# Expert lookup in two PSUM banks, and five edits where one block hands over to the next

## What is computed

```python
def adaln_norm(x, c, g, w_ada, b_ada):
    mod = jax.nn.silu(c) @ w_ada + b_ada
    shift, scale, gate = jnp.split(mod, 3, axis=-1)
    h = rms_norm(x, g) * (1.0 + scale[:, None, :]) + shift[:, None, :]
    return h, gate[:, None, :]

def peer(h, wq, subkeys, u_tab, v_tab):
    q = (xt @ wq).reshape(T, PEER_HEADS, 2, PEER_HALF)
    sc = jnp.einsum('thpd,hpkd->thpk', q, subkeys)
    vals, ids = lax.top_k(sc, PEER_TOPK)
    cand = (vals[:, :, 0, :, None] + vals[:, :, 1, None, :])
    cid = (ids[:, :, 0, :, None] * PEER_KEYS + ids[:, :, 1, None, :])
    top, pos = lax.top_k(cand, PEER_TOPK)
    idx = jnp.take_along_axis(cid, pos, axis=-1)
    g = jax.nn.softmax(top, axis=-1)
```

## Time and profile before

| | us |
|---|---|
| median of 3 runs | 2238.18 (2234.31 to 2246.16) |
| profiled execution | 2242.05 |
| its span, first to last instruction | 2240.2 |
| PE busy | 2175.6, 97% |
| DVE busy | 1571.8, 70% |
| POOL busy | 1241.3, 55% |
| ACT busy | 937.6, 42% |
| mean granted TensorE clock | 0.986 of 2.4 GHz |

### The profile page before, as it was taken

How to read it: one execution, slowest core, us unless ns; L and a number is a source line. 1 busy time by engine, 2 the same in 40 slices (tenths; PEclk the granted TensorE clock), 3 DMA queues, 4 the chain that set the end, 5 groups by cost and what they waited for, 6 DMA issues and landing times.

```text
span 2240.2 us, 32178 instructions
## 1 busy us (share of the span) xinstructions
PE 2175.6 (97%) x11877; PEld 1944.6 (87%) x11877; DVE 1571.8 (70%) x3061; ACT 937.6 (42%) x1541; POOL 1241.3 (55%) x670
## 2 busy tenths in 40 slices
PE   6999999999999999999999999999999999999999
PEld 6897989888888877888999999999998888888887
DVE  5736777685556755552999999999974766666665
ACT  3235576432455414432434334555553333333332
POOL 1634222375223341242588788766657787778775
PEclk9999999999999999999999999999999999999999
DMA  7252424222221440232488788999989999999995
GB/s 281 88 186 106 144 92 133 73 104 95 95 85 57 147 154 20 76 133 103 148 269 287 266 291 267 344 357 328 352 301 345 368 348 357 351 348 361 356 359 217
DMA packets 164476, 492.42 MB, mean 220 GB/s; under 512 B 15072, under 2 KB 64608, under 8 KB 162912
## 3 DMA queue, kind: packets, MB, share of 16 engines
q1 hardware_dynamic: 107872, 305.79, 39.3%
q0 software_dynamic: 36864, 134.23, 16.1%
q10 hardware_dynamic: 19584, 50.34, 5.9%
HBM read 437.87 MB, written 52.43 MB: 219 GB/s over the span
## 4 chain that ended last, share of the span: by engine, by line
PE 40%; DVE 9%; POOL 2%; DMA 1%; issue 1%; ACT 0%; DVEq 0%; ACTq 0%; POOLq 0%
PE ps L2566 22%; PE ps L2530 14%; PE ps L2548 4%; POOL t_split L2675 1%; DVE arena L2794 1%; DVE arena L2763 1%; DVE arena L2754 1%; DVE arena L2755 1%; DVE rope L2732 1%; DVE arena L2759 1%; DVE norm_rows L2732 1%; DVE arena L2789 1%; DVE arena L2732 1%; DVE arena L2750 1%; DVE arena L2797 0%
## 5 line engine op out<-in xcount | busy, mean ns | idle before, releaser
L2675 POOL TENSOR_TENSOR t_split<-t_raw,t_split 128x1024 fp32r<-128x1024 f32 x225 | 550.1, 2446 | 220.1 <-ACT t_split L2601 218.1
L267 POOL TENSOR_TENSOR w_split<-ring,w_split 128x1024 fp32r<-128x1024 f32 x113 | 274.3, 2428 | 490.9 <-ACT w_split L259 445.0
L2530 PE MATMUL ps<-h_hi,t_split 128*128 128x384 f32 x2048 | 537.4, 338 | 7.4 <-POOL t_split L2675 4.4
L2566 PE MATMUL ps<-t_split,w_split 128*128 128x512 f32 x2304 | 522.8, 389 | 3.1 <-DVE t_split L2849 1.6
L2566 PEld LDWEIGHTS ps<-t_split,w_split 128*128 128x128 f32 x2304 | 432.3, 188 | 93.5 <-DVE t_split L2849 2.0
L2601 ACT ACTIVATE t_split<-t_raw 128x1024 fp32r<-128x1024 f32 x256 | 270.3, 1057 | 340.2 <-PE ps L2566 304.0
L291 PE MATMUL ps<-h_hi,w_split 128*128 128x512 f32 x1280 | 402.6, 392 | 0.0
L2530 PEld LDWEIGHTS ps<-h_hi,t_split 128*128 128x128 f32 x2048 | 373.4, 189 | 10.1 <-POOL t_split L2675 6.6
L2530 PE MATMUL ps<-h_lo,t_split 128*128 128x384 f32 x1024 | 343.9, 336 | 0.0
L291 PEld LDWEIGHTS ps<-h_hi,w_split 128*128 128x128 f32 x1280 | 240.3, 188 | 50.5 <-issue 0.7
L291 PE MATMUL ps<-h_lo,w_split 128*128 128x512 f32 x640 | 249.1, 389 | 0.0
(11 more groups left out here) (367 smaller groups left out, 3333.3 us busy)
## 6 DMA issues: line engine op xcount, KB each, us to landing
ring<-w_stream SPq DMA_DIRECT2D x203, 512.0 KB, 3.4
t_raw<-u_table SPq DMA_DIRECT2D x128, 512.0 KB, 4.8
t_raw<-v_table SPq DMA_DIRECT2D x128, 512.0 KB, 5.6
gelu_scratch<-e_gel ACTq DMA_DIRECT2D x128, 192.0 KB, 4.8
gates_scratch<-arena ACTq DMA_DIRECT2D x8, 3072.0 KB, 13.4
arena<-gelu_scratch SPq DMA_DIRECT2D x32, 768.0 KB, 5.9
arena<-gates_scratch SPq DMA_DIRECT2D x32, 768.0 KB, 8.8
first<-w_stream SPq DMA_DIRECT2D x16, 512.0 KB, 13.3
```

What stands on the lines that cost most here:

```text
L267: pool.tensor_tensor(w_split[:, i % RS, 1, :], ring[:, n % R, :], w_split[:, i % RS, 0, :].bitcast(F32), ALU.subtract).then_inc(lo_done, 1)
L2530: mm = pe.matmul(ps[:, 6 + n % 2, 0:NT], t_split[:, n % RAWS, u, k * P:(k + 1) * P], h_parts[h][:, k, P:T], start=(k + u + h == 0), stop=( ...
L2566: mm = pe.matmul(ps[:, 2 * i + half, :], w_split[:, b % 2, w, at:at + P], t_split[:, m % RAWS, v, half * 512:(half + 1) * 512], start=(n + ...
L2675: pool.tensor_tensor(t_split[:, m % RAWS, 1, :], t_raw[:, m % RAWS, :], t_split[:, m % RAWS, 0, :].bitcast(F32), ALU.subtract).then_inc(t_ ...
```

## The change

It has these parts.

1. **Lookup**: the comparison and the product of the selection move from SBUF to banks 1 and 2 of PSUM (`match`), in place, in halves of 128 x 1024, with the comparison's 0..15 in bank 3. PE's turned selections all go to bank 0. The plan's prices go from 2.3, 2.3, 3.3 a pass to 1.2 a half pass.
2. **Shift's share**: DVE multiplies the weight piece with the shift and sums it over the tiles (`dve_share`, eight chained operations of 128 x 128, in SBUF), before it adds output unit 6; PE needs one matmul of one column instead of eight. The ring buffer of that piece waits for DVE's sum instead of PE's matmuls.
3. **Sums**: `pe_totals` runs inside the last output unit, ahead of its last two tiles; its part of DVE's chain is taken ahead (`dve_half`). The order of `dve_raw` moves up by one unit, and that of the raw products around the sums is changed.
4. **Two scaled tiles in PSUM**: tiles 2 and 3 of `dve_scale` go to bank 7 and to the bank of the shift; the copy of the shift's share comes between.
5. **`feature_group`** begins with the products of h's upper part and waits for the rest of h after them.
6. **Query norm**: the spreads, the rotations and one set of transposes in n2's phase come one unit later (spreads after units 7 to 9).
7. Two semaphores of one stage are merged into one (`f_dve`).

```diff
-                for k in range(KD):
-                    mm = pe.matmul(ps[:, self.shift_bank, 0:1], ring[:, n % R, k * P:(k + 1) * P],
-                                   self.shifts[:, k:k + 1], start=(k == 0), stop=(k == KD - 1))
-                mm.then_inc(self.turned.sem, 1)
+                self.share_summed.wait(pe, 1)
+                pe.matmul(ps[:, self.shift_bank, 0:1], share_sum, C("ones")[:, 0:1], start=True,
+                          stop=True).then_inc(self.turned.sem, 1)
...
+            def dve_share(self, dve):
+                n = self.raw_unit
+                dve.wait_ge(piece_in[n % R], 16 * (n // R + 1 - FIRST_PIECES // R))
+                for k in range(KD):
+                    block = ring[:, n % R, k * P:(k + 1) * P]
+                    if k == 0:
+                        ins = dve.tensor_scalar(share_sum, block, self.shifts[:, 0:1], None, ALU.mult)
+                    else:
+                        ins = dve.scalar_tensor_tensor(out=share_sum, in0=block, scalar=self.shifts[:, k:k + 1],
+                                                       in1=share_sum, op0=ALU.mult, op1=ALU.add)
+                    if k < KD - 1:
+                        dve.wait_ge(dve_step, note("dve", ins))
+                ins.then_inc(self.share_summed.sem, 1)
...
+            def scaled_tile(self, k):
+                if self.raw_unit is not None and k in (2, 3):
+                    return ps[:, 7 if k == 2 else self.shift_bank, :]
+                return ntmp[:, k, :]
...
-            if late:
-                for at in range(3):
+            if upper:
+                upper.wait(pe, 1)
+                for j in range(2):
+                    w[j] = piece_ready(pe, pieces[j])
+                    for a in range(2):
+                        pe.matmul(ps[:, banks[j], :], w[j][:, a, 0:P], src[0][:, 0, :], start=(a == 0), stop=False)
+                src_ready.wait(pe, 1)
+                for j in range(2):
+                    pe.matmul(ps[:, banks[j], :], w[j][:, 0, 0:P], src[1][:, 0, :], start=False, stop=False)
...
-                    feature_unit(pe, at + u, 4 + u % 3, h_parts)
+                    feature_unit(pe, at + u, 4 + u % 3, h_parts, pause=norm.pe_totals if u == KD - 1 else None)
...
-                    for v in {KD - 1: (KD - 3, KD - 2)}.get(u, (u - 2,) if u >= 2 else ()):
-                        norm.dve_raw(dve, v)
+                    if u >= 1:
+                        norm.dve_raw(dve, u - 1)
+                    if u == KD - 2:
+                        norm.dve_share(dve)
...
-                    for r in {6: (0, 1), 7: (2, 3), 8: (4,)}.get(u, ()):
+                    for r in {7: (0, 1), 8: (2, 3), 9: (4,)}.get(u, ()):
...
-                        step(dve.tensor_tensor(
-                            eq.rearrange("p h k a -> p (h k) a"),
-                            posab[:, j, :].unsqueeze(2).to_broadcast([P, P, PTOP]),
-                            C("iota16").unsqueeze(1).to_broadcast([P, P, PTOP]), ALU.is_equal))
-                        paced(2.3)
-                        step(dve.tensor_tensor(
-                            prod, eq, ids3[:, :, j, :].unsqueeze(2).to_broadcast([P, PH, PTOP, PTOP]), ALU.mult))
-                        paced(2.3)
-                        step(dve.tensor_reduce(sel[:, j, :], prod.rearrange("p h k a -> p (h k) a"), AX.X, ALU.add))
-                        paced(3.3)
+                        for half in range(2):
+                            of = slice(half * (P // 2), (half + 1) * (P // 2))
+                            heads = slice(half * (PH // 2), (half + 1) * (PH // 2))
+                            step(dve.tensor_tensor(
+                                match, posab[:, j, of].unsqueeze(2).to_broadcast([P, P // 2, PTOP]),
+                                iota_ps.unsqueeze(1).to_broadcast([P, P // 2, PTOP]), ALU.is_equal))
+                            paced(1.2)
+                            by_head = match.rearrange("p (h k) a -> p h k a", k=PTOP)
+                            step(dve.tensor_tensor(
+                                by_head, by_head, ids3[:, heads, j, :].unsqueeze(2).to_broadcast([P, PH // 2, PTOP, PTOP]),
+                                ALU.mult))
+                            paced(1.2)
+                            step(dve.tensor_reduce(sel[:, j, of], match, AX.X, ALU.add))
+                            paced(1.2)
```

## The result

| | before | changed |
|---|---|---|
| median, 10 runs each | 2244.64 us | 2255.45 us (2253.16 to 2263.28) |
| ratio, changed to before | | 1.0056, 95% interval 1.0039 to 1.0073 |
| profiled execution (span) | 2242.05 (2240.2) | 2253.16 (2251.3) |
| DVE busy | 1571.8 | 1565.5 |
| POOL busy | 1241.3 | 1226.3 |

The kernel became slower by 10.8 us; I had forecast 9.8 us less. The waits of PE say where to look. Each line names who waited, for whom, the sum in us, the number of waits and the longest.

The account below looks back on a forecast made before the run. PE, busy 97% of the span, was taken as the bound. 7.4 + 0.8 + 2.1 + 0.5 + 0.5 - 1.5 = 9.8 us gained, from 2238.2 to 2228.4 us; own range 2224 to 2234, with rivals 1 to 3 and noise 2217 to 2237.

Parts of the forecast that it names:

- lookup: Lookup: selection in PSUM shortens DVE's work, PE's waits for gelu and POOL go: 7.4 us gained, plus 0.8 of half clock.
- query spreads: Query norm in n2's phase: spreads one unit later, so DVE is no longer late: 2.1 us gained, 0 as other end.
- turn e: Turn e: 1.4 us gained at its end, 0.9 lost to DVE's later chain: net 0.5 us gained.
- turn f: Turn f: PE waits 2.4 us inside unit 7, half clock again: 1.5 us lost; without the low clock 1.1 gained.
- turn g: Turn g: same pattern as turn e, 0.5 us gained.
- Rival 2: Gates: PE waits for DVE, two more dot products among the comparisons; 4 us lost of the sum, 2232.5 us; chance 0.10.
- Rival 3: Lookup: only the exponential's wait goes, POOL stays late; the sum less 3.5, 2232 us; chance 0.10.
- The issues: Lookup: POOL's DMA issues, up to 2.8 us beside two-input DVE operations, would all be near 0.95 us.
- The half clock at the gates: Gates: 3.4 us at half clock, 1.6 us lost, may or may not go; half counted, 0.8 us gained.
- Rival 1: Turns: POOL's lock doesn't hold the share's operations; turns give 1.2 + 1.2 + 3.5, time 2222.0 us; chance 0.25.
- Rival 4: Lookup: PSUM operations run at half speed, 2.3 us each; 22 us slower, 2260 us; chance 0.05.

Follow-up runs that it names:

- old_prices: Changed kernel with the plan's prices of a half pass at 1.15, 1.15 and 1.65, the sum of before; 2229.02 us, ratio 0.9930 to the kernel before.
- lookup_priced: Kernel before with only the lookup moved to PSUM and the plan's sum of prices as before; 2232.50 us, ratio 0.9949.
- share_psum: `old_prices` with the partial sums of the shift's share in bank 7 of PSUM; 2226.64 us, ratio 0.9940.
- both_mended: `share_psum` with the third selection turned over after tile 70 and not 71; 2222.40 us, ratio 0.9900.
- dots_55: `both_mended` with `paced(4.3)` ahead of the gates, so 55 dot products stand before the first comparison; 2227.10 us, ratio 0.9912.
- sums_behind: `both_mended` with the sums of the first seven tiles back behind output unit 7, ahead of the raw products; 2226.49 us, ratio 0.9914.
- lookup_alone: Kernel before with part 1 of the change only (lookup in PSUM, prices 1.2, 1.2, 1.2); 2253.62 us, ratio 1.0049.
- turns_alone: Changed kernel with part 1 undone, the lookup back in SBUF; 2239.13 us, ratio 0.9978.

## Why the prediction was wrong, by its own steps

| term, us (- is gained) | forecast | measured |
|---|---|---|
| lookup | -8.2 | +7.9 (-8.4 up to the third turnover, +16.3 behind it); -10.8 with the old sum of prices |
| query spreads | -2.1 | -2.1 wait; stretch from the sums to the windows 107.5 to 104.1, with 2.7 less at half clock at its end |
| turn e | -0.5 | -0.05 |
| turn f | +1.5 | +0.7 |
| turn g | -0.5 | -0.9, of it 0.6 half clock |

**The lookup is the step that failed**, and in it one sentence: "DVE has some two dot products more to do beside the gates; one between the third and fourth comparison may cost PE 0.4 us". I had counted the two dot products that move, and had DVE's end at 1381.2 and PE's place of the turnover in front of me. I had put together only that DVE "was already idle", not that its idle time grows from 3.07 us to 16.89, nor what stands behind the comparison it idles at. In place of the 0.4 us the runs showed POOL held for 12.59 us behind dot product 51, PE idle for 7.09 us, and 10.24 us at half clock: 10.0 us lost between the turnover and the first gates. The row below is from the kernel before; it was the one to ask "and if this becomes five times as long?".

```profile
1384.24 0.69 DVE L2823 TENSOR_TENSOR arena<-ps,arena 128x512 f32<-128x512 f32 x1 [3.07 <-ACT arena L2619]
```

Rival 2 came nearest: it had the right dot products, but saw them as too much work for DVE among the comparisons. They were too late for POOL. Rival 3, that POOL stays late in the old places, is out: its waits there are gone. The forecast of 2228.4 us is close to what `old_prices` takes (2229.02), but partly by luck: the kernel before had a median of 2243.29 beside it where I reckoned from 2238.2, so it gained 14.3 us for my 9.8, of them 10.8 in the lookup where I had 8.2. What was right: the durations, the waits that vanish (the gelu's, POOL's but for 1.0 us at the start) and, in `old_prices`, the issues all near 0.95 us.

**The issues.** In the kernel before nine of POOL's 128 gathers took 2.8 us for 0.95, and each of the nine began beside a two-input operation of the selection and ended 0.82 us after it. One is that at 1366.84, beside the comparison of 1364.53 to 1368.84:

```profile
1366.84 2.83 POOL L2686 DMA_INDIRECT rope<-u_rows,arena  x1 [0.16 <-issue]
```

With the selection in PSUM the longest in `old_prices` is 1.12 us. In the changed kernel one still took 2.83, and it ended 0.82 us after the sum of candidates (L2810), the two-input operation of this size that was left in SBUF. The Trainium skill, "SBUF — State Buffer", section "Who interferes with whom", infers that a `tensor_tensor` doesn't hold up the making of descriptors; these rows are against it.

**The half clock at the gates** didn't go but grew to 10.24 us behind the 7.09 us of idle PE. In `old_prices` there is none at this place.

**Turns e and g**: the lock held the share as forecast (4.82 us for seven operations; I had 2.3 behind a held one of 2.5), PE waited 0.63 us (0.7 forecast), the rest of tile 2 took 0.74 us. Short operations took 0.35 us each, not 0.29. The small gain of 0.5 came out as 0.05 in e.

**Turn f**: PE waited 1.83 us (2.4 forecast). From the last matmul of the attention's weights (`prob_dil`) to the first sums of the query norm it takes 99.3 us before and 100.0 in the changed kernel, with half clock in the turn in both (6.83 and 3.41 us) and the same 6.83 us ahead of it: +0.7. `lookup_priced`, the old program here, has neither stretch and takes 93.2 us: the two cost it some 6.0. In the turn itself the seven profiles with the share in SBUF all show 3.41 us at half clock, the four with it in PSUM (`share_psum`, `both_mended`, `dots_55`, `sums_behind`) none, and the old program has it in two of three. That PE's wait for the sums beside the short matmuls brings it on fits this and isn't shown by it.

**Rival 1**, that the share isn't held, is refuted for this code. **Rival 4** (PSUM at half speed, 2.3 us an operation) as well: 1.23 us. I had asked how a *slower* lookup on DVE would hurt, and the slower side came from a faster one.

**What stays open.** The lookup of the profiled execution explains 7.9 of the 10.8 us, and `lookup_alone` shows that the lookup alone can make up the whole loss (10 us). In the ten runs of the changed kernel the mean clock lay between 0.979 and 0.983, in those of `turns_alone` between 0.984 and 0.989; 10 us more at half clock in the lookup explain 0.002 of it. Whether the extra half clock up to 390 us comes more often in one program than in another, and why, no run here tells.

## What to carry to other kernels

When an engine gets faster, look for the first wait in its list that another engine's fixed place sets, and at what stands behind it in the same list: that work will not get earlier with it, and whoever needs it (here POOL's gather, and in POOL's own queue the table splits) is late. A planner's prices are not only durations: they place work, and a price corrected to the truth moves instructions. Test such a plan on both sides, and compare stages and not totals where executions differ by 8 us at the same program.

## What was not expected of the hardware

An operation of 128 x 128 with its partial sum in PSUM takes 354 to 356 ns, and with all in SBUF 351 to 352 when it isn't held, 2496 when it is; and 128 x 1024 in place in PSUM takes 1.23 us for compare, product and sum alike. PSUM as a scratch for elementwise work cost nothing here. All ten long POOL issues of the two kernels ended 0.82 us after a DVE operation with two inputs in SBUF. And the same instructions up to turn e take 390.3 to 398.1 us in 14 profiles, with 20.5 to 47.8 us of them at half clock.
